# Softmax normalisation of the attention units moved from a transposed reciprocal on the output to a scaling of the probabilities on GpSimd

## The reference

```python
def row_block(r):                      # one of 16 grid rows, 16 heads of width 64
    rs = row_start[r]                  # 8 key rows around r
    s = jnp.einsum('bhqd,bhrkd->bhqrk', qb, kb).astype(jnp.float32) * scale + bias
    s = jnp.where(col_in[:, None, :], s, -jnp.inf)         # 16 key columns around each query
    s_ctx = jnp.einsum('bhqd,bhcd->bhqc', qb, kc).astype(jnp.float32) * scale
    p = jax.nn.softmax(jnp.concatenate([s.reshape(B, NA_HEADS, GRID_W, kr * GRID_W), s_ctx], axis=-1), axis=-1)
    p_lat = p[..., :kr * GRID_W].reshape(B, NA_HEADS, GRID_W, kr, GRID_W)
    return jnp.einsum('bhqrk,bhrkd->bhqd', p_lat, vb) + jnp.einsum('bhqc,bhcd->bhqd', p[..., kr * GRID_W:], vc)
```

## Time and profile before

| what | value |
|---|---|
| median of 3 runs (lowest, highest) | 3051.69 us (3050.55, 3053.93) |
| the profiled execution | 3053.93 us, its span 3052.1 us |
| PE matmul busy | 2938.6 us, 96% of the span |
| DVE busy | 1578.0 us, 52% |
| ACT busy | 1050.5 us, 34% |
| POOL busy | 296.7 us, 10% |
| attention loop, first to last transposes of a unit | 1737.7 to 2163.4 us |

### The profile page before, as it was taken

The page is one execution under the profiler, slowest core; times in us unless marked ns, Lnnn a source line. Parts: engine busy times, 40 slices in busy tenths (PEclk is TensorE's granted clock), DMA queues, the critical chain, the costliest instruction groups (busy, mean ns, idle before and its releaser), DMA issues. The chain is left out here.

```text
span 3052.1 us, 38095 instructions
## 1 busy us (share of the span) xinstructions
PE 2938.6 (96%) x15863; PEld 2407.1 (79%) x15863; DVE 1578.0 (52%) x1879; ACT 1050.5 (34%) x1265; POOL 296.7 (10%) x287
## 2 busy tenths in 40 slices
PE   5899999999999999999999999999799999999998
PEld 3787787878888888888888877778677888888886
DVE  5668567264454445454472255555436444445445
ACT  5586875141121221121142344444323222222223
POOL 3121230200000000000033300000010000000002
PEclk7999999999999999999999999999899999999998
DMA  7443334222212111211223433332511111111111
GB/s 281 128 129 100 117 95 147 64 78 75 69 56 69 63 56 62 70 59 54 68 76 97 135 80 92 88 80 67 182 49 42 56 42 49 49 49 43 47 49 56
DMA packets 259846, 249.19 MB, mean 82 GB/s; under 512 B 45707, under 2 KB 230619, under 8 KB 253531
## 3 DMA queue, kind: packets, MB, share of 16 engines
q1 hardware_dynamic: 247835, 192.62, 20.9%
q0 software_dynamic: 11776, 54.13, 5.5%
q10 hardware_dynamic: 64, 0.01, 0.0%
HBM read 212.45 MB, written 31.26 MB: 80 GB/s over the span
## 5 line engine op out<-in xcount | busy, mean ns | idle before, releaser
L706 PE MATMUL ps<-zH,wH 128*128 128x512 f32 (+1 forms) x2048 | 751.3, 367 | 5.9 <-ACTq L1092 4.5
L706 PE MATMUL ps<-zL,wH 128*128 128x512 f32 (+1 forms) x2048 | 749.0, 366 | 0.0
L706 PE MATMUL ps<-zH,wL 128*128 128x512 f32 (+1 forms) x2048 | 748.4, 365 | 0.0
L706 PEld LDWEIGHTS ps<-zH,wH 128*128 128x128 f32 x2048 | 386.8, 189 | 86.1 <-issue 13.8
L706 PEld LDWEIGHTS ps<-zH,wL 128*128 128x128 f32 x2048 | 386.7, 189 | 62.6
L706 PEld LDWEIGHTS ps<-zL,wH 128*128 128x128 f32 x2048 | 386.9, 189 | 62.3
L2235 DVE SCALAR_TENSOR_TENSOR res<-ps,mod,res 128x1024 f32<-128x1024 f32 x240 | 236.7, 1014 | 186.5 <-PE ps L706 175.5
L716 DVE SCALAR_TENSOR_TENSOR V<-ps,vec,V 128x1023 f32<-128x1023 f32 x126 | 128.1, 1016 | 369.5 <-ACT V L2094 366.5
L2067 ACT ACTIVATE wH<-wraw 128x1024 fp32r<-128x1024 f32 x130 | 134.8, 1052 | 388.4 <-PE ps L706 388.4
L706 PE MATMUL ps<-hH,wH 128*128 128x512 f32 (+1 forms) x700 | 260.2, 372 | 0.3 <-DVE res L2235 0.3
L706 PE MATMUL ps<-hL,wH 128*128 128x512 f32 (+1 forms) x700 | 258.5, 369 | 0.0
(11 more groups left out here) (320 smaller groups left out, 4893.3 us busy)
## 6 DMA issues: line engine op xcount, KB each, us to landing
wraw<-in_ffn_w_up_dram SPq DMA_DIRECT2D x88, 512.0 KB, 3.9
modw<-in_mod_w_dram POOLq DMA_DIRECT2D x40, 1024.0 KB, 5.1
wraw<-in_ffn_w_down_dram SPq DMA_DIRECT2D x44, 512.0 KB, 3.3
wraw<-in_na_w_in_dram SPq DMA_DIRECT2D x32, 512.0 KB, 4.0
bias<-scratch_bias SPq DMA_DIRECT2D x512, 32.0 KB, 1.8
modring<-in_mod_w_dram SPq DMA_DIRECT2D x8, 1024.0 KB, 14.3
wraw<-in_rg_w_in_dram SPq DMA_DIRECT2D x16, 512.0 KB, 4.6
v<-scratch_v SPq DMA_DIRECT2D x128, 64.0 KB, 2.1
```

The source lines that it names most:

```text
L706: last = nc.tensor.matmul(ps[:, slot * SLOT + c:slot * SLOT + c + n], w(k), r(k)[:, c:c + n], start=(k == 0 and i == 0), stop=(k == K - 1 ...
```

## The change

The division moves from the output to the probabilities. `inverse(g)` now makes just two numbers a row, `rowstat` columns 4 and 5. A new step on POOL, `scale(g)`, waits for it and multiplies each head's S (608 or 640 columns) by its number in place. `turn(g)` on PE waits for that step (`scaled`) instead of `exp_done`, and the transpose of `share` is gone. ACT's copy of the rest has 256 columns instead of 384 and goes into the fifth chunk of `pT`, which has one buffer where `rest` had two. `out(g)` is a copy. POOL's `w_low` for the blocks from 20 on now stands between the `scale` steps, after `scale(g)` of unit 1 and of unit 4 in each pair.

```diff
-    m.pT = w.put("pT", [P, 2, NCH - 1, P])
-    m.rest = w.put("rest", [P, 2, 3 * P])
-    m.share = w.put("share", [P, 2, P])
+    m.pT = w.put("pT", [P, 2, NCH, P])
...
     def gpsimd(gp):
+        def scale(g):
+            gp.wait_ge(recip, g + 1)
+            for hd in range(2):
+                x = m.S[:, g % 2, hd, 0:WIDTH[g % 2]]
+                nc.gpsimd.tensor_scalar(x, x, m.rowstat[:, g % 2, 4 + hd:5 + hd], None, ALU.mult).then_inc(scaled, 1)
...
-        for n in range(3, BLOCKS):
+        for n in range(3, 20):
             w_low(gp, n)
+        for g in range(NT):
+            i, it = divmod(g, NR)
+            scale(g)
+            if it == 1:
+                w_low(gp, 20 + 2 * i)
+            elif it == 4:
+                w_low(gp, 21 + 2 * i)
...
         def turn(g):
             for hd in range(2):
-                pe.wait_ge(exp_done, 2 * g + hd + 1)
+                pe.wait_ge(scaled, 2 * g + hd + 1)
...
             for hd in range(2):
-                transpose(g, hd, MAIN)
-            pe.wait_ge(recip, g + 1)
-            nc.tensor.transpose(ps[:, SHARE_AT:SHARE_AT + P], m.share[:, g % 2, :], m.ident[:, :]).then_inc(t_done, 1)
+                ins = transpose(g, hd, MAIN)
+            ins.then_inc(t_done, 1)
...
-            nc.scalar.activation(m.rest[:, g % 2, :], ps[:, REST_AT:REST_AT + 3 * P], ACT.Copy).then_inc(pT_act, 1)
+            nc.scalar.activation(m.pT[:, :, MAIN, :], ps[:, REST_AT:REST_AT + 2 * P].rearrange("p (h q) -> p h q", h=2), ACT.Copy).then_inc(pT_act, 1)
...
-            nc.vector.reciprocal(m.share[:, g % 2, :].rearrange("p (h d) -> p h d", h=2),
-                                 m.rowstat[:, g % 2, 2:4].unsqueeze(2).to_broadcast([P, 2, DH])).then_inc(recip, 1)
+            nc.vector.reciprocal(m.rowstat[:, g % 2, 4:6], m.rowstat[:, g % 2, 2:4]).then_inc(recip, 1)
...
-            sums, share = [x.rearrange("p (r c) -> p r c", c=QC) for x in (ps[:, O_AT:O_AT + P], m.rest[:, g % 2, 2 * P:3 * P])]
-            nc.vector.tensor_tensor(grid(m.oT[i % 2][:, :])[:, QR * h:QR * h + QR, QC * cb:QC * cb + QC], sums, share, ALU.mult).then_inc(o_ready, 1)
+            nc.vector.tensor_copy(grid(m.oT[i % 2][:, :])[:, QR * h:QR * h + QR, QC * cb:QC * cb + QC],
+                                  ps[:, O_AT:O_AT + P].rearrange("p (r c) -> p r c", c=QC)).then_inc(o_ready, 1)
```

More of the change, by code:

```diff
@@ L2376, in attention @@
     v_in, ctx_in, bias_in = [sem(f"na_v_in{i}") for i in range(3)], [sem(f"na_ctx_in{i}") for i in range(2)], [sem(f"na_bias_in{i}") for i in range(2)]
-    s_done, s_biased, exp_done, recip = [sem("na_" + n) for n in ("s_done", "s_biased", "exp_done", "recip")]
+    s_done, s_biased, exp_done, recip, scaled = [sem("na_" + n) for n in ("s_done", "s_biased", "exp_done", "recip", "scaled")]
     t_done, pT_act, pT_dve, o_done, o_ready, o_out = [sem("na_" + n) for n in ("t_done", "pT_act", "pT_dve", "o_done", "o_ready", "o_out")]
@@ L2394, in attention @@
     REST_AT = 6 * BANK
-    SHARE_AT = 6 * BANK + 2 * P
-    O_AT = 6 * BANK + 3 * P
+    O_AT = 6 * BANK + 2 * P
     FILL_BANK = 7
@@ L2647, in values @@
                     p0 = DH * hd
-                    ins = nc.tensor.matmul(ps[p0:p0 + DH, O_AT:O_AT + P], v[:, p0:p0 + DH], (m.pT[0:n, hd, c, :] if c < MAIN else m.rest[0:n, g % 2, hd * P:(hd + 1) * P]), start=(c == 0), stop=(c == NCH - 1))
+                    ins = nc.tensor.matmul(ps[p0:p0 + DH, O_AT:O_AT + P], v[:, p0:p0 + DH], m.pT[0:n, hd, c, :], start=(c == 0), stop=(c == NCH - 1))
             ins.then_inc(o_done, 1)
```

## The result

The changed kernel took 3068.89 us (median of 4 runs, 3067.81 to 3069.94), the kernel before 3051.12 beside it. The ratio is 1.0058, with a 95% interval of 1.0044 to 1.0074: 17.8 us slower, where 7.0 us faster was forecast. Measured again later it was 3066.51 us, ratio 1.0057 (1.0044 to 1.0069).

A forecast was written before the change was run, and what follows sets the result against it. PE's work bounds the first seven pairs, SP's bias queue part of the last; -6.4 for transposes and -0.6 for the tail make -7.0 us, median 3044.7 us. Own range 3043 to 3046.5, eight in ten 3043 to 3055.

The forecast's parts named there:

- The new step, its size: POOL's scaling of one head's S, 640 columns: taken as 0.85 us, range 0.64 to 1.62.
- T: POOL's time to scale one head's S; taken as 0.85 us, hidden everywhere below 1 us.
- the sum: -6.4 us for the transposes and -0.6 for the tail: -7.0 us, median 3044.7 us.
- (b): Scaling queued behind POOL's weight block: 2T - 2.08 in unit 5, 2T - 2.91 in unit 2, if positive; forecast zero.
- (a): Ordinary unit: at least 1.60 + 2T, 3.3 us, between units' head 1; units 6.61 and 7.35 apart, so no cost.
- (c): Units without `fill`: unit 55 loses nothing below T = 0.96, unit 63 nothing below 0.98; no cost forecast.
- rival B: POOL at its two-input pace, T = 1.6, its queue becomes what PE waits for: +5.7 us, 3057.4 us; chance 0.12.
- The transposes: Missing share transposes on PE's path, units 0 to 55: 0.115 us each, 6.4 us gained.
- ACT's shorter copy and DVE's reciprocal: Copy 0.12 us less, hidden in the loop, counting in the last two units; reciprocal 0.94 to 0.159 us, worth nothing.
- `out` as a copy: DVE's output step: as long as before, bound 0 to 0.1 us a unit, at most 1.3 in all, taken as 0.
- The tail: Last units: shorter copy and missing transpose count together, 0.24 us each, unit 61's share 0.16; 0.6 us gained.
- Rival C: Transposes are worth nothing, because PE gains waits elsewhere as it gets faster: 3051.7 us; chance 0.08.

The follow-up runs named there:

- run of forms: Changed kernel with another form of POOL instruction in each pair of heads, durations only; pair 1, one multiplication by a constant, took 1.81 us.
- the first experiment: Changed kernel with POOL's scaling step left out, output not normalised; 3043.47 us, ratio 0.9976 to the kernel before.

## Why the prediction was wrong

The step that failed is "The new step, its size": T = 0.85 us, with 0.64 and 1.62 as its ends. It was 1.887 and 1.807. The one-input operation next to it, the affine select, was a different instruction with its own pace. The two-input row was no upper end: on the same 640 columns tensor_tensor took 1.25 us and the single multiplication 1.88. That 0.85 lies near another form of the same multiplication, 0.80, is luck: nothing in its working told the forms apart.

The Trainium skill ("GPSIMD Engine Reference", Performance versus the Vector engine) gives 1.8 cycles an element at its best, 0.96 us for 640 columns as an estimate, and calls one-input work roughly line-rate (Engine selection). The form with two multiplications, 0.80, is even under that estimate; the one that the change uses, 1.887, is twice it and slower than the two-input tensor_tensor, and the measurement decides.

The rest of the sum can be checked at three sizes of T. At 0.80 it gives -7.0 us, and -8.6 and -7.7 were measured. At 1.25 it gives -3.4, and -7.4 was measured: it overstates what a small excess costs. At 1.85, (b) gives 10.2 + 4.2 = 14.4, and the loop from 0 to 54 is 14.15 us longer than without scaling. That they agree is partly luck. By the distances between the units, unit 5 costs 9.3 us, unit 2 3.4 and unit 7 1.5: (b) overstates its two places by 1.8 us, and the sum lacks the third, where (a) had said nothing is lost in the first seven pairs. At the forecast T of 0.85 that was right; it fails above (5.11 - 1.60)/2 = 1.76. The run of forms bears this out: at the constant's T of 1.81, unit 7 of pair 1 lost 0.11 us, which is 1.60 + 2 x 1.81 - 5.11. For (c), the formulas of rival B give 2124.66 + 3.75 + 8 x 5.27 = 2170.6 for head 1 of unit 63, 7.9 us later than before, which is what the last pair of the trace shows. In all -6.4 + 14.4 + 7.9 = +15.9 us, against +17.8 and +16.7. So rival B was the right mechanism, with both of its places, and I had cut off its price by a bound that didn't hold.

The transposes: nearly right, 5.80 us over 54 units without scaling, so 0.107 each and not 0.115. ACT's shorter copy and DVE's reciprocal: no cost or gain of their own on the path, as said (the reciprocal has 0.15 us; `out` as a copy 0.288, as before). The tail: 0.6 us forecast, 2.5 measured in unit 54 to 63 without scaling. Up to 1 us of it lies in SP's queue, whose 16 bias pieces of step 30 took 7.49 us there and 8.25 before. Much of the rest goes with the clock, 0.95 there and 0.91 before; the two traces of the scaling on DVE lie about 2 us apart beyond their waits for the bias. The 1.78 us of ten transposes in the earlier trace rows fall into this slower stretch as well. How the 2.5 us divide is not shown. Rival C falls with the first experiment.

## What to carry to other kernels

The duration of an instruction form that the trace doesn't hold is unknown on POOL, and the nearest rows are not its bounds: measure it alone first, in several spellings, since the spelling was worth a factor of 2.35. Before a step goes to an idle engine, work out the loop that it closes (here 1.60 + 2T between units) and the longest instruction that can stand ahead of it in the queue; the engine's idle share says nothing about either. A DVE that loses an operation can take the new one at the same place: two instructions of 0.551 us here, against two of 0.805 in POOL's fast form and of 1.887 in the form of the change. And where PE stands idle for long, as in the last pair, read the clock of each trace before a difference of some us is given to the change.

## What the runs showed of the hardware

- POOL, 640 float32 columns in place: copy 0.72 us; two constant multiplications 0.725; multiplication and multiplication or addition with the row's number 0.80; both by the row's number 0.875; tensor_tensor of the tensor with itself or with the broadcast number 1.25; one multiplication or addition with the row's number 1.88, one multiplication by a constant 1.81; two additions 2.42. At 256 columns the single multiplication took 0.922, so 2.5 ns a column and about 0.28 us fixed.
- After one and the same short wait of PE the clock fell in one trace and not in another. In the second trace of the changed kernel the wait of 1.20 us, there in the first too, was followed by a fall of the granted clock in unit 5 of pair 0:

```profile
1740.00:1770.00 30.00, 29.14 (x248) 23.22 (x248) 11.95 (x33) 13.40 (x28) 18.30 (x10) 1.00 0.27 64
1770.00:1800.00 30.00, 28.26 (x212) 22.08 (x211) 11.52 (x30) 12.13 (x27) 15.76 (x9) 0.94 0.33 85
```

```profile
1774.90 1.34 PE L2621 MATMUL ps<-ident,S 128*128 128x128 f32 x6 [1.20 <-POOL S L2574]
...
1776.89 0.63 PE L2675 MATMUL ps<-zH,wL 128*128 128x512 f32 x1
...
1779.06 0.39 PE L2675 MATMUL ps<-zH,wL 128*128 128x512 f32 x1
```

  Six transposes took 1.34 us instead of 0.88 and a matmul of `fill` 0.63 instead of 0.39. The clock was 0.94 over these 30 us, so it was at the lower of its two levels (1.2 instead of 2.4 GHz) for 12% of them, and 0.97 over 1980 to 2040, where unit 5 of pair 4 lies; the distance from unit 5 to 6 grew by 1.6 us in each of these two pairs. Units 0 to 54 took 396.40 us in this trace and 393.26 in the first, where the clock stayed at 1.00. The same program with the same waits got both; what decides is not shown.
- The 16 bias issues of SP's queue took between 7.29 and 8.9 us within each of five traces (up to 8.62 in that of the kernel before), in slow waves over some hundred us, with no change in the code. In the last pair, where they set the pace, that could move the time by about a microsecond (an estimate; no run isolates it).
- With the scaling on DVE, PE waited 2.2 us in the last pair of one trace and the clock stayed at 1.00; it waited 3.0 us in the other, the clock fell, and the same stretch of the same kernel took 39.20 us instead of 36.15, of which 0.8 are a longer wait for the bias pieces. With the weight blocks on DVE the clock was 0.94 in that stretch with no wait of PE over 1.2 us. What decides is not shown here either.
